# The even mixing phase of a two-layer decoder step, its RWKV part in chunks of 64 tokens, with the output projection's pieces late in the step

## The reference, cut to what matters

```
p = rmsnorm(h) @ w_in                      # input projection
o_ret  = retention(q, k, v)                # 4 heads, chunked, with a state matrix
# RWKV-7 part, 8 heads of width 64, one step per token:
S = S * exp(lw_t) - (S @ kk_t) (kk_t * a_t)^T + v_t k_t^T
y_t = S @ r_t
y = groupnorm(y) * ln_w + ln_b + (sum(r * k * r_k)) * v
out = concat(o_ret * silu(rg), y * silu(gb)) @ w_out      # output projection, 1024 x 1024
h = h + out
```

## Time and profile before

| | |
|---|---|
| runs of the kernel before | 3101.29 us median of 3 (3094.16 to 3106.37) |
| the profiled execution | 3103.8 us, its span 3101.8 us |
| PE busy in the span | 2999.8 us, 97% |
| DVE, ACT, POOL busy | 1930.9, 1003.0, 503.7 us |
| mean granted clock of TensorE | 0.98 |
| even mixing phase, 712 to 1567 us | PE busy 816.23 of 855 us, DVE 610.63, ACT 309.04, POOL 304.94 |

### The profile page before, as it was taken

One profiled execution on the slowest core, in us unless ns is written; L12 is line 12 of the kernel. 1 busy time (PEld: TensorE's weight loads), 2 busy tenths in 40 slices (PEclk: granted clock), 3 DMA queues, 4 the chain that ended last, 5 costly groups with the idle time before them and its releaser, 6 DMA issues. The chain is left out here.

```text
span 3101.8 us, 89481 instructions
## 1 busy us (share of the span) xinstructions
PE 2999.8 (97%) x38740; PEld 2724.6 (88%) x38740; DVE 1930.9 (62%) x4060; ACT 1003.0 (32%) x2220; POOL 503.7 (16%) x519
## 2 busy tenths in 40 slices
PE   9999999996999999999989999999997999999998
PEld 8999999996888887888789999999995688888886
DVE  5212344445777777777445156776765688888886
ACT  5211210003343343343167122222223344444441
POOL 0000000001333333343300000000001111111112
PEclk9999999998999999999899999999998999999999
DMA  8421221215233433433353221221214223333333
GB/s 260 120 87 60 74 75 63 67 50 175 73 109 114 121 115 106 121 120 108 108 197 115 67 71 61 77 78 60 77 50 156 77 84 99 97 100 97 96 104 130
DMA packets 227704, 311.69 MB, mean 100 GB/s; under 512 B 34793, under 2 KB 166129, under 8 KB 227185
## 3 DMA queue, kind: packets, MB, share of 16 engines
q1 hardware_dynamic: 213840, 260.30, 26.4%
q0 software_dynamic: 9152, 29.94, 3.3%
q10 hardware_dynamic: 4320, 15.73, 1.8%
HBM read 210.18 MB, written 95.72 MB: 99 GB/s over the span
## 5 line engine op out<-in xcount | busy, mean ns | idle before, releaser
L414 DVE SCALAR_TENSOR_TENSOR po_stage<-po_work,po_cw,po_stage 128x424 f32<-128x424 f32 (+1 forms) x360 | 232.1, 645 | 28.3 <-issue 1.7
L595 PE MATMUL po_ps<-po_xnT_hi,po_w_hi 128*128 128x424 f32 x960 | 205.0, 355 | 0.0
L595 PE MATMUL po_ps<-po_xnT_hi,po_w_lo 128*128 128x424 f32 x960 | 204.4, 355 | 0.0
L595 PE MATMUL po_ps<-po_xnT_lo,po_w_hi 128*128 128x424 f32 x960 | 204.1, 354 | 0.0
L299 ACT ACTIVATE po_work<-po_ps 128x424 f32<-128x424 f32 (+1 forms) x120 | 61.7, 514 | 407.9 <-PE po_ps L595 407.9
L595 PEld LDWEIGHTS po_ps<-po_xnT_hi,po_w_hi 128*128 128x128 f32 x960 | 180.2, 188 | 5.2
L595 PEld LDWEIGHTS po_ps<-po_xnT_hi,po_w_lo 128*128 128x128 f32 x960 | 180.4, 188 | 4.5
L595 PEld LDWEIGHTS po_ps<-po_xnT_lo,po_w_hi 128*128 128x128 f32 x960 | 180.2, 188 | 4.6
L595 PE MATMUL pe_ps<-pe_w_hi,pe_xnT_hi 128*128 128x256 f32 x1088 | 153.8, 284 | 5.5 <-ACT pe_xnT_hi L299 5.2
L595 PE MATMUL pe_ps<-pe_w_lo,pe_xnT_hi 128*128 128x256 f32 x1088 | 153.5, 284 | 0.0
L595 PE MATMUL pe_ps<-pe_w_hi,pe_xnT_lo 128*128 128x256 f32 x1088 | 153.3, 284 | 0.0
(11 more groups left out here) (463 smaller groups left out, 7140.4 us busy)
## 6 DMA issues: line engine op xcount, KB each, us to landing
me_ring<-scratch_w_lo SPq DMA_DIRECT2D x68, 512.0 KB, 3.9
mo_c<-scratch_ch_o SPq DMA_DIRECT2D x51, 512.0 KB, 3.7
scratch_ch_o<-po_stage SPq DMA_DIRECT2D x96, 212.0 KB, 1.9
scratch_tok_e<-pe_stage SPq DMA_DIRECT2D x136, 128.0 KB, 1.9
pe_raw<-in_w_in_e POOLq DMA_DIRECT2D x52, 256.0 KB, 4.3
me_xs<-scratch_ch_e SPq DMA_DIRECT2D x17, 768.0 KB, 6.8
po_raw<-in_w_in_o POOLq DMA_DIRECT2D x48, 256.0 KB, 4.0
scratch_ch_e<-pe_stage SPq DMA_DIRECT2D x52, 212.0 KB, 1.9
```

The lines of the kernel that those rows point to most:

```text
L414: return nc.vector.scalar_tensor_tensor(out=o, in0=a, scalar=s, in1=b, op0=op0, op1=op1)
L595: last = nc.tensor.matmul(out, left.bitcast(F32R), right.bitcast(F32R), start=(i == 0 and k == 0), stop=(i == 2 and k == KD - 1))
```

## The change

The RWKV part keeps its tiles of 128 tokens but computes inside them in two chunks of CK = 64, one after the other; retention stays in tiles of 128.

- Products of keys and scores are made only inside a chunk: for each head two 64 x 64 blocks (`with_own_chunk`), keys and receptances in one matmul with 128 columns. `key_side` is one call, `receptance_scores` is gone (its values come with `key_scores` of the step before, and `G2T` gets two buffers). The levels end at b = 32; `TB`, `low_block` and the level 64 are gone.
- `right_side`/`outputs_of_values` become `values_part` (32 matmuls of 64 x 64 with 64 columns) and `from_state` once per chunk (8 matmuls with contraction 128, 64 rows and 128 columns). The outputs of chunk 0 go to rows 64 to 127 of `C_` and those of chunk 1 to rows 0 to 63; ACT copies them back (`outputs_of_values`).
- The solve, its scaling, the state increments and the state update are made once per chunk: state_new of chunk 0 is waited for by `from_state(t, 1)`, state_new of chunk 1 by the next tile.
- ACT takes over the copy of the right side; its key factors go behind the exponentials, and the tangent of the low-rank inputs from before to behind the copies of turned queries and keys and of pair sums.
- PE's order is new. Of the eight projection pieces one stays early in the step and seven come behind `outputs_of_solved`.
- DVE's order follows: `factors` earlier, both residual halves at the end, `mixed` behind `low_products`.
- POOL: the bonus is gated before the next keys, queries are scaled behind `mix_retention`, two clearings of `TF` and `TB` are gone.

The diff, cut to its core:

```diff
+CK = 64
-            return [b for b in LEVELS[1:] if b < (DEC_T if n == PT else P)]
+            return [b for b in LEVELS[1:] if b < (DEC_T if n == PT else CK)]
...
+            def right_side(t, c):
+                at = rows_of(c)
+                await_chunk(act, "rhs_ready", t, c)
+                A(rhs[at], heads(A_, WN)[at], ACT.Copy).then_inc(E["rhs_copied"], 1)
+            def outputs_of_values(t):
+                await_(act, "y_ready", t)
+                await_(act, "mixed", t - 1)
+                A(yb[0:CK], heads(C_, WN)[CK:P], ACT.Copy)
+                A(yb[CK:P], heads(C_, WN)[0:CK], ACT.Copy).then_inc(E["y_copied"], 1)
...
-            def new_state(t):
-                await_(dve, "y_ready", t)
+            def new_state(t, c):
                 for half in range(2):
                     s = s_wk[64 * half:64 * half + 64, :, half, :]
-                    await_(dve, f"delta{half}_ready", t)
+                    await_chunk(dve, f"delta{half}_ready", t, c)
                     tt(s, s, heads(D_, WN)[64 * half:64 * half + 64, 0:4, :], AD)
                 dve.drain()
-                await_(dve, "fac_ready", t)
+                await_(dve, "fac_ready", t + c)
-                tt(s, s, bc(fac[t % 2][:], 2 * WN), M).then_inc(E["state_new"], 1)
+                tt(s, s, bc(fac[t % 3][:, c], 2 * WN), M).then_inc(E["state_new"], 1)
...
+            def from_state(t, c):
+                at, over = rows_of(c), rows_of(1 - c)
+                await_chunk(pe, "state_new", t - 1 + c, 1 - c)
+                for b in range(4):
+                    ...
+                    last_op = mm(A_[at, cols], l[0], r, start=False, stop=b == 3)
+                    mm(C_[over, cols], l[1], r, start=False, stop=False)
+            def values_part(t):
+                ...
+                for h in range(H):
+                    for w, bank in enumerate((A_, C_)):
+                        for c in range(2):
+                            at = rows_of(c)
+                            mm(bank[rows_of(c ^ w), cols], MG[at, h, w, :], tokV[t % 2][at, h, :], ...)
+            def state_of_chunk(t, c):
+                for left, right in ((tokK, tokV[t % 2]), (tokB, wv)):
+                    if left is tokB:
+                        await_chunk(pe, "wv_ready", t, c)
+                    for b in range(4):
+                        for half in range(2):
+                            ... mm(D_[p0:p0 + 64, ...], left[t % 2][at, b, p0:p0 + 64], right[at, 2 * b + half, :])
+            def with_own_chunk(n, which, banks, event):
+                for b in range(4):
+                    for k, bank in enumerate(banks):
+                        p0 = 64 * k
+                        for c in range(2):
+                            at = rows_of(c)
+                            last_op = mm(bank[at, b * P:(b + 1) * P], BK[p0:p0 + 64, which, b, at], KR[n % 2][p0:p0 + 64, :, b, at])
```

More of the change, by code:

```diff
@@ L675, in even_block_tables @@
     low = [((t[:, None] // seg == t[None, :] // seg) & (t[:, None] < t[None, :])).astype(np.float32) for seg in (P, DEC_T)]
-    return np.concatenate([block_tables()] + [np.tile(m, (P // Q, 1)) for m in low], 1)
+    side = [np.repeat(np.arange(P // Q) % 2 == k, Q)[:, None].astype(np.float32) for k in range(2)]
+    return np.concatenate([block_tables()] + [np.tile(m, (P // Q, 1)) for m in low] + [np.tile(m, (P // Q, 1)) * k for m in low + [np.ones((Q, Q))] for k in side], 1).astype(np.float32)
 def pair_table():
@@ L768, in mix_even_phase @@
         XA = sb("XA", [P, H, Q])
[L769 to L772, removed]
+        TF = sb("TF", [P, H, CK])
+        G2T = sb("G2T", [P, 2, H, CK])
+        MG = sb("MG", [P, H, 2, CK])
+        spare = [sb(f"spare{j}", [P, D]) for j in range(2)]
         qk = sb("qk", [P, 8, RDK])
@@ L886, in level_count, with turn_count @@
             return LV[n] + levels_of(n).index(b) + 1 if b in levels_of(n) else None
+        def turn_count(n, b):
+            return sum(len([c for c in levels_of(i) if c < Q]) for i in range(n)) + levels_of(n).index(b) + 1
         def await_(eng, name, n):
@@ L1284, in _ @@
                     log_decays(m)
-                    key_factors(m)
+                if t is not None:
+                    right_side(t, 0)
                 if n is not None:
@@ L1292, in _ @@
                     exponentials(m)
-                if t is not None:
-                    squared_retention(t)
+                    squared_keys(m)
+                    key_factors(m)
+                if t is not None and t < PT:
+                    right_side(t, 1)
                 if n is not None:
@@ L1319, in _ @@
                 if n is not None:
[L1320 to L1321 removed]
+                    level(n, 32)
                 if q is not None:
@@ L1604, in _ @@
                 if t is not None:
-                    solved(t)
+                    solved(t, 0)
+                if m is not None:
+                    raw_keys(m)
+                if n == 0:
+                    split_weights(3)
+                if t is not None and t < PT:
+                    new_state(t, 0)
                 if n is not None:
+                    turn_blocks(n, 2)
                     mask(n, 4)
+                if n == 0:
+                    split_weights(4)
+                    split_weights(5)
                 if m is not None:
@@ L1610, in _ @@
                 if t is not None and t < PT:
-                    new_state(t)
-                if n == 0:
-                    split_weights(4)
-                    split_weights(5)
+                    solved(t, 1)
                 if n is not None:
                     turn_blocks(n, 4)
+                    mask(n, 8)
+                if n == 0:
+                    split_weights(6)
+                    split_weights(7)
+                if m == 1:
+                    dve.wait_ge(s_wl[3], 16)
+                if m is not None:
+                    factors(m)
+                if t is not None and t < PT:
+                    new_state(t, 1)
+                if n is not None:
+                    masked(n)
                 if t is not None:
@@ L2023, in _, with beside @@
                 last_step = p == PT
-                if t is not None:
-                    right_side(t)
-                if n == 0:
-                    keep_clock(8)
+                def beside(count, *parts):
+                    if p is not None and not last_step:
+                        for part in parts:
+                            project(p, part)
+                    elif p is None and n is not None:
+                        keep_clock(count)
                 if n is not None:
@@ L2030, in _ @@
                 if t is not None:
-                    outputs_of_values(t)
+                    values_part(t)
+                    from_state(t, 0)
                 if n == 0:
```

557 lines of the change are left out of this document (230 added, 327 removed).

## The result

| | before | after |
|---|---|---|
| median of 4 runs | 3103.83 us (3094.16 to 3111.51) | 3139.73 us (3132.83 to 3142.30) |
| profiled execution, its span | 3103.8, 3101.8 us | 3139.8, 3137.8 us |
| forecast | | 3028 us, 3003 to 3082 |

The account below looks back on a forecast made before the run. PE's own work was taken to bound the even mixing phase at 44.95 us a step; 4.3 less over 16 steps (69 us) and 5 for the sample tile gave 3030 profiled, stated as 3028 us, range 3003 to 3082.

Parts of the forecast that it names:

- Work of PE: Even mixing phase, per step: 16.9 us of PE work removed, 11.6 added, so 5.3 us less.
- rival 1: `values_part`, `outputs_of_solved`: row halves sharing a bank don't overlap; +2.1 us a step, 3062 us; chance 0.06.
- rival 2: All four-place packing fails, `with_own_chunk` too: +4.3 us a step, 3097 us, no change that counts; chance 0.04.
- 40.65: Forecast us per step in the even mixing phase: 44.95 - 5.3 + 1.0 of new waits.
- The chain over two chunks: State through DVE twice a step: PE waits 0.25 at `from_state(t, 1)`, 0.15 at `key_side`, 0.25 at `level_T` 32.
- Rival 3: Seven places depending on DVE each wait 0.3 us more: 2.1 us a step, 3062 us; chance 0.18.
- The walk of DVE's queue: DVE ready at 36.3, so `turn_mix` at 36.4 waits 0.1 us for `mixed`; no slack from `low_products` to `split_mix`.
- rival 4: Clock falls early in the step until pieces 1 and 2: +7.7 us a step, 3151 us, slower; chance 0.08.
- gap of 1.70 us: Sign cited for rival 4: this gap among small products was followed by the lower clock, with PE busy.
- my 5 us for the sample tile: Sample tile's `right_side` and `outputs_of_values`, 10.3 us at the lower clock, take about half; saves 5, between 0 and 8.

Follow-up runs that it names:

- e7: Changed kernel with projection pieces spread over the step and `mixed` ahead of the block masks on DVE: 3094.22 us, ratio 0.9982 to the kernel before.
- e6: Changed kernel with `mixed` and attention ahead of the block masks on DVE: ratio 1.004 to the kernel before.
- e13: Kernel before plus a burst of small and long products, without semaphores, at the end of the even mixing phase: blocks of 128 records start 3.68 us apart.
- e15: Same burst as e13, beside the step's channel loads (768 KB, two in flight): 5.4 us a block, 24 records a us.
- e2: Changed kernel with twelve more 512-column products in the first half of each step: ratio 1.012 to the kernel before.
- e5: Changed kernel with levels 2 to 16 made for four of eight heads only, 256 records a step fewer: ratio 0.9766 to the kernel before.
- e12: Same kernel as e6, run again for its profile: ratio 1.0046 to the kernel before.
- e9: e7 with `split_mix` ahead of the residual halves on DVE and piece 5 beside 6 on PE: 3085.8 us, ratio 0.995 to the kernel before.
- e3: Changed kernel with most of three data loads (channels, values, residual's input) left out for prompt tiles: ratio 1.0053 to the kernel before.

## Why the prediction was wrong

**Work of PE: right.** Forecast 16.9 removed, 11.6 added. Start to start in the timeline after, `values_part` takes 1.10 us (1.2), `from_state` 1.02 (1.18), a solve 1.05 (1.08), each half of the increments 0.46 to 0.56 at the full clock (0.61). `outputs_of_solved` takes 1.07 (1.2) and `key_side` 0.94 (1.1). 32 products of 64 x 64 over all four places and two banks in 1.10 us refute rival 1, and `key_side` refutes rival 2. The rule of the Trainium skill (TensorEngine Tiling (Array Packing), "Restrictions and Gotchas") that row tiles can't use one bank at once doesn't hold for these: at one after the other by row half they would have taken 2.4. Busy time is 40.7 us a step where 39.2 was forecast (40.65 less 1.5 of waits). In e7, with the same products and the clock at 0.99, a step takes (675.0 - 10.2) / 15 = 44.3 us (state decays from 800.6 to 1475.6, the last two 10.2 apart) and PE is busy 444.30 / 500 of it, 39.4; so 1.3 of the 1.5 are the clock. (From start to start the new groups take some 10.4 us at the full clock, not 11.6. Busy time doesn't show this gain: it also counts the tail of the record ahead of each wait, 0.19 us and more, and there are about six waits a step.)

**The chain over two chunks: right.** Waits for the state, the scaling and the inverse together are 0.6 us a step, forecast 0.7 for these. Rival 3 didn't come.

**`turn_mix`: mis-sized.** Forecast 0.1, measured 1.6 us. The walk of DVE's queue had no reserve from `low_products` to `split_mix`, as I wrote, and I still gave it 0.1. e6 shows the price, 22 us of time.

**The failed step: "The other groups, the projection's eight pieces among them, are moved only, at no price on PE."** The sum had no term for the arrival of PE's instructions, neither for the order nor for the number of small products. The new order puts some 700 records of small products in a row with one piece between, and keeps the long ones together at the end. The stream brings 35 records a us, and 24 beside the loads (e13, e15). What the two kernels ask for, in the densest five us of a step (PE busy with its records, clock, DMA share, GB/s), first the kernel before, then the one after:

```profile
1111.00:1116.00 5.00, 5.00 (x171) 1.00 0.61 187
```

```profile
1091.00:1096.00 5.00, 4.29 (x202) 1.00 0.02 3
```

171 / 5 = 34 a us is at the stream's rate, for five us and with quieter ones around it. 202 / 4.29 = 47 is above it, and so PE ran dry. That costs 3.9 us a step more than before. Taken apart by runs: e2, filling at little cost; e5, 4.3 us a step back for 256 records; and with `mixed` early in both, spreading the pieces (e12 to e7) takes the issue waits from 4.3 to 1.8 us a step and the busy time from 41.5 to 39.4, while 2.3 us of waits for `mixed` and `mixT_lo` come back, so that 18 us are left by the medians. So some 2.5 us of issue waits are the order of the pieces. The 1.3 us above the kernel before that e7 keeps are not; the chunks' own many small products are the likely cause, but no run takes them apart. And with the pieces spread the change is still no gain (0.9982).

**The clock: rival 4 in its form, not in its cause.** I let the clock fall for narrow products that keep the array idle, and priced it at 7.7 us a step. It fell behind gaps, to 0.50 for some us, and cost about 1.3: each of its 15 falls between 800 and 1500 us came during a wait of PE or within 2.4 us of one's end. In e7 it falls six times there and is 0.99 from 900 to 1400 us, with the same products and shorter gaps. I had the sign of this in hand: the earlier trace rows show a gap of 1.70 us that is put down to issue, and the earlier trace rows six such waits. I took them as given instead of asking what ends them.

**The sum.** Issue +3.9, `mixed` and other waits +1.2 over the forecast, busy time +1.5 (clock 1.3): 6.6 of the 6.7 us a step over 40.65, 107 us over 16 steps. The profiled forecast of 3030 and these 107 make 3137, measured 3139.8. That is closer than it deserves: the next phase starts 104 us later than forecast (1602.9 for 1572.6 - 69 - 5), and the other 6 us lie in the phases behind it. From the last decay to the next phase it is 82.2 us, 91.7 before, but the last decay now lies later in its step, so how much of my 5 us for the sample tile came isn't shown.

**Open.** Why e9 and e7 still wait 1.8 to 2 us a step for issue though a step as a whole asks for 23 records a us. The spacing of the transfers, never below 3.2 us, with 178 records at hand at most where it can be read, speaks for little being fetched ahead, so that quiet parts of a step don't pay for dense ones; no run varies it. And how much of after's gaps is contention: e3 gives 19 us for it, but it takes away other uses of those loads too. No version tried keeps the gain that the work alone would bring, 5.3 us a step.

## What to carry to other kernels

Count instructions as well as time: for each stretch of PE's queue, records per us, against what the trace shows that the stream delivers (35 here, 24 beside heavy loads). Long products between groups of small ones are not filler, they are the time in which the next instructions arrive; moving them has a price even if PE's work is the same. A gap inside a group of identical matmuls, with "issue" as its end, is neither a semaphore nor an engine, and its distance to the next such gap, a multiple of 128 records or nearly so (127 in the step above), with an instruction transfer that lands shortly before its end, tells what it is.

## What the runs showed of the hardware

- PE's instructions came in transfers of 16.4 KB on the queue that the profile calls instruction, one per 128 matmul records with their 128 weight loads: 64 bytes each. One arrived every 3.68 us when nothing else moved, every 5.4 us beside loads at a DMA share of 0.99. PE went on 1.2 to 1.6 us after the landing, and no two transfers of any trace here start less than 3.2 us apart.
- The Trainium skill (Trainium Architecture — The Big Picture, "The software stack") says in its list of what happens to a kernel that the instruction streams are moved to the engines when the program is loaded. By this trace that list isn't the whole: 317 such transfers lie inside the execution.
- The rate doesn't depend on PE's clock: 35 records a us at 0.50 and at 1.00 granted clock (e13).
- The clock was at 0.50 through the pure burst, where PE was busy half of the time, and fell behind single gaps of 1.4 and 1.5 us in the step (those that end at 1126.70 and 1320.63).
